# Two dense stages whose last round is handed over tile by tile, with other warming products on TensorE

## What is computed

```python
# block 1
x = x + g1 * (merged @ w_out[l])
h2 = rms_norm(x, norm2_gain[l]) * (1.0 + sc2) + sh2
x = x + g2 * moe_ffn(h2, w_router[l], ...)      # 32 experts, top 4 of 32, 1024 -> 2x1024 -> 1024
...
# block 2
x = x + merged @ w_out[l]
h2 = rms_norm_2(x, norm_ffn_g[l]).reshape(B * S, D)
y = hierarchical_moe(h2, ...)                   # 4 groups of 8 experts, top 1 group, top 2 inside, 1024 -> 256 -> 1024
x = x + y.reshape(B, S, D)
```

## Time and profile before

| what | value |
|---|---|
| median of three runs | 1577.53 us |
| lowest and highest of them | 1576.42 and 1578.69 us |
| span of the profiled execution | 1575.5 us |
| TensorE busy | 1455.8 us (92%) |
| VectorE, ScalarE busy | 602.0 us (38%), 339.3 us (22%) |
| mean granted TensorE clock | 0.985 |
| read from HBM | 592.66 MB, 377 GB/s over the span |

### The profile page before, as it was taken

One profiled execution on the slowest core, in us unless ns is written; L12 is line 12 of the kernel. 1 busy time (PEld: TensorE's weight loads), 2 busy tenths in 40 slices (PEclk: granted clock), 3 DMA queues, 4 the chain that ended last, 5 costly groups with the idle time before them and its releaser, 6 DMA issues.

```text
span 1575.5 us, 20915 instructions
## 1 busy us (share of the span) xinstructions
PE 1455.8 (92%) x8704; PEld 758.2 (48%) x8704; DVE 602.0 (38%) x911; ACT 339.3 (22%) x391; POOL 20.8 (1%) x33
## 2 busy tenths in 40 slices
PE   5999999999999999999999999999989999997677
PEld 2878985333333333333333333333348999753343
DVE  4686683232222231322313223223257587322111
ACT  4564432010101110101101001011033474221110
POOL 2100100000000000000000000000000000000000
PEclk9999999999999999999999999999999999998899
DMA  9976599999999999999999999999985437899997
GB/s 382 366 262 265 197 357 379 428 428 428 427 429 427 428 429 427 428 428 428 427 428 429 425 429 428 428 430 427 429 331 190 169 124 295 358 421 422 422 422 315
DMA packets 76733, 594.59 MB, mean 377 GB/s; under 512 B 5354, under 2 KB 6592, under 8 KB 37252
## 3 DMA queue, kind: packets, MB, share of 16 engines
q1 hardware_dynamic: 74416, 588.25, 90.4%
q0 software_dynamic: 1728, 4.86, 1.0%
q10 hardware_dynamic: 532, 0.64, 0.1%
HBM read 592.66 MB, written 1.06 MB: 377 GB/s over the span
## 4 chain that ended last, share of the span: by engine, by line
PE 50%; DMA 42%; DVE 6%; issue 1%; ACT 1%; SPq 0%; DVEq 0%; ACTq 0%
PE PS L539 45%; DMA ring<-in_w_up 32%; DMA ring<-in_w_gate_e 7%; PE PS L708 3%; DMA ring<-in_w_ada 1%; DMA arena<-in_w_in 1%; DVE ring_r L349 1%; PE PS L732 1%; PE PS L648 0%; DVE arena L807 0%; PE PS L1456 0%; ACT ring_r L344 0%; DVE arena_r L349 0%; PE PS L568 0%; DVE arena L2010 0%
## 5 line engine op out<-in xcount | busy, mean ns | idle before, releaser
L539 PE MATMUL PS<-ring,arena 128*64 128x512 f32 x3020 | 670.8, 596 | 46.2 <-DMA ring<-in_w_up 38.5
L539 PEld LDWEIGHTS PS<-ring,arena 128*64 128x64 f32 x3020 | 209.8, 137 | 469.5 <-issue 389.1
L539 PE MATMUL PS<-arena 128*128 128x128 f32 (+12 forms) x1240 | 227.6, 441 | 4.8 <-ACT arena L535 1.4
L795 DVE TENSOR_SCALAR arena<-PS 128x512 f32<-128x512 f32 x32 | 22.1, 692 | 487.6 <-PE PS L539 487.6
L539 PE MATMUL PS<-ring_r 128*128 128x256 f32 (+1 forms) x576 | 171.4, 305 | 0.4 <-DVE ring_r L1935 0.3
L518 ACT ACTIVATE arena<-arena 128x512 f32<-128x512 f32 x32 | 20.2, 630 | 703.3 <-DVE arena L795 703.3
L539 PEld LDWEIGHTS PS<-arena 64*128 64x128 f32 (+6 forms) x1240 | 108.4, 165 | 121.8 <-issue 114.4
L539 PE MATMUL PS<-hT_r,ring_r 128*128 128x256 f32 x800 | 151.4, 285 | 1.1 <-DVE ring_r L349 1.1
L349 DVE TENSOR_TENSOR ring_r<-ring,ring_r 128x2048 fp32r<-128x2048 f32 x51 | 116.4, 2291 | 39.3 <-ACT ring_r L344 38.2
L539 PEld LDWEIGHTS PS<-hT_r,ring_r 128*128 128x128 f32 x800 | 127.4, 193 | 3.2 <-issue 2.3
L344 ACT ACTIVATE ring_r<-ring 128x2048 fp32r<-128x2048 f32 x51 | 97.2, 1911 | 103.5 <-PE PS L539 98.5
(11 more groups left out here) (374 smaller groups left out, 974.8 us busy)
## 6 DMA issues: line engine op xcount, KB each, us to landing
ring<-in_w_up SPq DMA_DIRECT2D x128, 2048.0 KB, 23.2
ring<-in_w_down SPq DMA_DIRECT2D x59, 2048.0 KB, 21.6
ring<-in_w_in SPq DMA_DIRECT2D x17, 2048.0 KB, 11.2
ring<-in_w_gate_e SPq DMA_DIRECT2D x14, 2048.0 KB, 20.9
ring<-in_w_up_e SPq DMA_DIRECT2D x14, 2048.0 KB, 19.6
ring<-in_w_down_e SPq DMA_DIRECT2D x14, 2048.0 KB, 20.2
ring<-in_w_ada SPq DMA_DIRECT2D x12, 2048.0 KB, 15.9
ring<-in_w_out SPq DMA_DIRECT2D x4, 2048.0 KB, 7.7
```

Source lines behind the costliest of these rows:

```text
L539: return nc.tensor.matmul(o, w, m, start=first, stop=last)
L795: V.tensor_scalar(glu.rearrange("p (kk b q) -> p kk b q", kk=4, b=2), hu[:, :, :, :, 0], 7.0, None, ALU.min)\
```

## The change

It touches the end of both dense stages. The last round gives tile 0 to VectorE as soon as tile 0's products are done; the transposes of the first half move between the products of tile 0 and those of tile 1; the second half goes tile by tile through product, sum, gain, transposes, root and copies. Four warming products go in two places of the first tail, four in one place of the second, and there two wide and four short ones become seven short. The third group of position sums goes to bank 4 and gets a signal of its own.

```diff
@@ semaphores
+        OUT_ENDS = (R2 - 1, len(ROUNDS) - 1)
-            return S("half_done"), 1 + sum(1 for p in PIECES[:n] if not p[1])
+            return S("half_done"), 1 + sum(1 for p in PIECES[:n] if not p[1]) + (n >= M0)
+        def first_tile_done(r):
+            return S("half_done"), piece_used(pieces_of(r)[0])[1] + 1
@@ TensorE, split_tokens
+                        if r in OUT_ENDS and last and i == 0:
+                            ins.then_inc(S("half_done"), 1)
+                            after_first()
@@ TensorE, transposes in place of transpose_half
+        def transpose_first(pe, n):
+            pe.wait_ge(S("h"), H_SEEN[n] + 1)
+            src = h if n == "n2" else z4
+            for i in range(TT):
+                for k in range(4):
+                    last = nc.tensor.transpose(PS[:, i, k * P:(k + 1) * P], src[:, i, k * P:(k + 1) * P], ident)
+            last.then_inc(S("h_transposed"), 1)
+        def transpose_second(pe, i, n):
+            pe.wait_ge(S("h"), H_SEEN[n] + 2 + i)
+            src = h if n == "n2" else z4
+            for k in range(4):
+                last = nc.tensor.transpose(PS[:, 2 + i, k * P:(k + 1) * P], src[:, i, (4 + k) * P:(5 + k) * P], ident)
+            last.then_inc(S("h_transposed"), 1)
@@ TensorE, first tail
-            split_tokens(15, merged1_low)
+            split_tokens(15, merged1_low, None, lambda: transpose_first(pe, "n2"))
-            transpose_half(pe, 0)
             pe.wait_ge(S("shift_products"), 1)
             mm(PS[:, 6, 480:512], C("ones"), shift_sums, True, True).then_inc(S("logits"), 1)
-            keep_warm_short(4, 7)
+            transpose_second(pe, 0, "n2")
             pe.wait_ge(S("hT_A"), 2)
             for i in range(TT):
                 router_mm(w_r1, NE, i, range(4))
-            transpose_half(pe, 1)
-            keep_warm_short(4, 7)
+            transpose_second(pe, 1, "n2")
@@ TensorE, second tail
-            transpose_half(pe, 0, "n4")
-            keep_warm_short(4, 7)
+            transpose_second(pe, 0, "n4")
...
-            transpose_half(pe, 1, "n4")
+            transpose_second(pe, 1, "n4")
...
-            keep_warm(2, 7)
-            keep_warm_short(4, 7)
+            keep_warm_short(7, 7)
@@ TensorE, positions_mm
-            mm(PS[:, 5, 64:96], C("before"), M[:, 1, :], False, True)
-            mm(PS[:, 5, 128:160], C("ones"), M[:, 0, :], True, False)
-            mm(PS[:, 5, 128:160], C("ones"), M[:, 1, :], False, True).then_inc(S("positions"), 1)
+            mm(PS[:, 5, 64:96], C("before"), M[:, 1, :], False, True).then_inc(S("positions"), 1)
+            mm(PS[:, 4, 128:160], C("ones"), M[:, 0, :], True, False)
+            mm(PS[:, 4, 128:160], C("ones"), M[:, 1, :], False, True).then_inc(S("positions"), 1)
@@ ScalarE, rms_end in place of rms_sums
+            for tile in range(TT):
+                act.wait_ge(S("x_ready"), X_SEEN[n] + 2 + tile)
+                square(1, tile)
+                if tile == 0:
+                    root(0)
+                second_half(tile)
+            root(1)
@@ VectorE, first tail, second half of the columns
+            c = slice(512, 1024)
+            for i in range(TT):
+                xt_i = xt[:, 512 * i:512 * (i + 1)]
+                wait(v, first_tile_done(15) if i == 0 else (S("big_done"), 16))
+                last = TV(xt_i, PS[:, banks(15).start + i, :], G1[:, c], ALU.mult)
...
+                sig(TV(x[:, i, c], x[:, i, c], xt_i, ALU.add), "x_ready")
+                sig(TV(h[:, i, c], x[:, i, c], A2[:, c], ALU.mult), "h")
+                if i == 0:
+                    mean("n2", 0)
+            for i in range(TT):
+                if i:
+                    mean("n2", 1)
+                inverse_root("n2", i)
+                v.wait_ge(S("h_transposed"), T_SEEN["n2"] + 2 + i)
+                L(STT(out=h[:, i, :], in0=h[:, i, :], scalar=sm("rs")[:, i:i + 1], in1=SH2, op0=ALU.mult, op1=ALU.add))
```

More of the change, by code:

```diff
@@ L484, in gate_sig, with rms_end, square, root @@
                 .then_inc(S("big_free_A"), 1)
-        def rms_sums(act, n, squares, between=None):
-            k = int(n[1])
-            nc.scalar.sqrt(sm("nm")[:, 0:1], C("ones")[:, 0:1])
[L491 to L505, removed]
+        def rms_end(act, n, squares, first_half, second_half):
+            def square(i, tile):
+                a = 4 * i + 2 * tile
+                nc.scalar.activation(squares[:, a:a + 2, :] if squares is not None else
+                                     PS[:, (0 if i else 4) + tile, :].rearrange("p (k n) -> p k n", k=2),
+                                     x[:, tile, 512 * i:512 * (i + 1)].rearrange("p (k n) -> p k n", k=2),
+                                     ACT.Square, accum_out=sm("ss")[:, 2 * i + tile:2 * i + tile + 1])\
+                    .then_inc(S("squares"), 1)
+            def root(tile):
+                act.wait_ge(S("mean_square"), RMS_SEEN[n] + 1 + tile)
+                nc.scalar.sqrt(sm("rs")[:, tile:tile + 1], sm("ss")[:, tile:tile + 1]).then_inc(S("rms"), 1)
+            nc.scalar.sqrt(sm("nm")[:, 0:1], C("ones")[:, 0:1])
+            act.wait_ge(S("x_ready"), X_SEEN[n] + 1)
+            for tile in range(TT):
+                square(0, tile)
+            act.wait_ge(S("h_transposed"), T_SEEN[n] + 1)
+            first_half()
+            if squares is None:
+                act.wait_ge(S("hT_A"), 2)
+            for tile in range(TT):
+                act.wait_ge(S("x_ready"), X_SEEN[n] + 2 + tile)
[4 more added lines that the diff above has]
+            root(1)
@@ new lines, in mean, with inverse_root @@
+            def mean(name, tile):
+                ss = sm("ss")
+                v.wait_ge(S("squares"), (5 if name == "n2" else 11) + tile)
+                L(TV(ss[:, tile:tile + 1], ss[:, tile:tile + 1], ss[:, 2 + tile:3 + tile], ALU.add))
+                sig(TS(ss[:, tile:tile + 1], ss[:, tile:tile + 1], 1.0 / D, EPS, ALU.mult, ALU.add), "mean_square")
+            def inverse_root(name, tile):
+                v.wait_ge(S("rms"), RMS_SEEN[name] + 1 + tile)
+                L(V.reciprocal(sm("rs")[:, tile:tile + 1], sm("rs")[:, tile:tile + 1]))
@@ L2432, in _, with scaled @@
             split_lower(v, M0 + 27)
[L2433 to L2441 removed]
+            c = slice(0, 512)
+            gain4 = at(A2MAP, "gain")
+            o = begin(R2 + 14)
+            sig(TV(x[:, :, c], x[:, :, c], o, ALU.add), "big_free_V")
+            sig(V.memset(sm("ang"), 0.0), "x_ready")
+            v.wait_ge(S("ffn_gain"), 16)
+            sig(TV(z4[:, :, c], x[:, :, c], bc_mid(gain4[:, c], TT), ALU.mult), "h")
+            c = slice(512, 1024)
+            for i in range(TT):
+                wait(v, first_tile_done(R2 + 15) if i == 0 else (S("big_done"), len(ROUNDS)))
+                sig(TV(x[:, i, c], x[:, i, c], PS[:, banks(R2 + 15).start + i, :], ALU.add), "x_ready")
+                sig(TV(z4[:, i, c], x[:, i, c], gain4[:, c], ALU.mult), "h")
+                if i == 0:
+                    mean("n4", 0)
+            sig(V.memset(sm("ang"), 0.0), "big_free_V")
+            def scaled(i):
+                inverse_root("n4", i)
+                v.wait_ge(S("h_transposed"), T_SEEN["n4"] + 2 + i)
+                return TS(h[:, i, :].rearrange("p (k q) -> p q k", k=KD), z4[:, i, :].rearrange("p (q k) -> p q k", k=KD),
+                          sm("rs")[:, i:i + 1], None, ALU.mult)
+            L(scaled(0))
+            v.wait_ge(S("h_transposed"), T_SEEN["n4"] + 3)
             sig(CP(hT[:, 4:8, P:256], PS[:, 3, :].rearrange("p (k n) -> p k n", n=P)), "hT_V")
[L2443 to L2446 removed]
+            mean("n4", 1)
+            L(scaled(1))
             logits(3, "b_r2", 36)
```

89 lines of the change are left out of this document (35 added, 54 removed).

## The result

| | kernel before | changed kernel |
|---|---|---|
| median | 1577.3 us (20 runs) | 1581.79 us (20 runs) |
| lowest and highest | 1574.68 and 1579.13 | 1575.43 and 1583.73 |
| ratio of the times, 95% interval | | 1.0028 [1.002, 1.0036] |
| profiled execution: time, span | span 1575.5 us | 1582.97 us, span 1581.1 us |

The change makes the kernel slower by 0.28%. The forecast was no change, 1577.4 us; the measured time lies inside its range and beyond the bound of 0.2%, on which the lower end of the interval lies. The runs of the changed kernel fall into two heaps: three lie at 1575.43, 1576.16 and 1576.85, and the other seventeen between 1580.5 and 1583.73. The runs of the kernel before form one heap. The profiled execution, at 1582.97 us, belongs to the seventeen.

A forecast was written before the change was run, and what follows sets the result against it. The prediction took the weight loads to bound both expert stages. First tail -1.0 and second tail +0.85 gave -0.15 us on the span of 1575.5; with runs 2.0 us above it, the forecast was 1577.4 us, range 1575.4 to 1582.5.

The forecast's parts named there:

- What bounds the kernel: Both expert stages: each ends when its stream of weight loads ends; first-tail gains count up to 4.6 us.
- First tail at full clock: End of the first dense stage: logits 0.70 us earlier, tail 1.0 us shorter, bounds 0.5 and 1.3.
- The load that waits for the dense end: SyncE's load issued at 234.44 in the first tail: moves 1.05 us later, counted as nothing.
- the hole: Pause in the weight loads behind the first tail: 4.6 us before, forecast 3.6 us after the change.
- Second tail: End of the second dense stage: transposes delay the dense products and loads by 1.05 us; net cost 0.85 us.
- 0.2 us given back: Second tail: faster work behind the dense products regains only 0.2 us, the loss at the second stage's first slot.
- The clock: First tail: forecast held it at 1.00; rivals had it fall for some 7 us (0.27) or longer (0.13).
- the rival to which it gave 0.27 and 0.13: Clock falls in the first tail: 1580.1 us if for some 7 us (0.27), 1583.3 if longer (0.13).
- the short case: First tail: clock low for 6.8 us, back when the gather starts; price 2.7 us, 1580.1 us; chance 0.27.
- The long case: First tail: clock stays low through the gather's 32 instructions, 3.2 us more, 1583.3 us; chance 0.13.
- Tile 0 early: First tail: VectorE does tile 0 2.8 us ahead; rival without it 1579.5 us, 0.06 with other small losses.
- both tails counting: Rival: TensorE bounds the second expert stage, so both tails' gains count, -1.0 - 4.0, 1572.5 us; chance 0.04.

The follow-up runs named there:

- e2: Changed kernel with both groups of four warming products put back in the first tail; 1577.21 us, ratio 1.0004.
- e7: Changed kernel with four warming products added in the first tail, only behind the transposes of tile 1; 1577.95 us, ratio 1.0.
- e8: Changed kernel with eight identity transposes in each of two first-tail places, ahead of tile 0's second-half transposes and behind tile 1's; 1577.5 us, ratio 1.0002.
- e11: Changed kernel with twelve warming products instead of seven between router and position sums of the first tail; 1577.18 us, ratio 1.0003.
- e3: Kernel before without its two groups of four warming products in the first tail, order by halves kept; 1582.02 us, ratio 1.0029.
- e10: Changed kernel with the second tail's first-half transposes moved behind the last dense product, no warming group back; 1582.07 us, ratio 1.0032.
- e1: Changed kernel with four warming products put back in the first tail, ahead of tile 0's second-half transposes; 1578.03 us, ratio 1.0009.

## Why the prediction was wrong

**What bounds the kernel: right.** Both expert stages end with their streams of loads. The whole loss of the first tail passes through to the end: +4.25 at the first slot's load, +5.6 at the end of the span with the second tail's share.

**First tail at full clock: right.** Forecast were 0.70 us at the logits and 1.0 us in all. Without a fall the tail measures 17.89 to 18.09 us, with 1.05 added 18.94 to 19.14, against 19.94 before: 0.8 to 1.0 us shorter. These are kernels with warming products added (e2, e7, e8, e11); the changed kernel itself wasn't profiled without a fall. The load that waits for the dense end was costed at nothing, with the hole as its cover, and the cover held, since this sum is counted at the end of the hole. Something was lost ahead of it: 344 GB/s in the window 236 to 240 us of the changed kernel and 381 in e11, against 430 before. In e11 the hole itself, reckoned as in the prediction, was (276 + 10 + 6) x 4 / 428 = 2.7 us, and 0.4 us more were lost in that window; forecast were 3.6.

**Second tail: right.** Forecast was +1.05 for the dense end, measured +0.95; forecast were 0.2 us given back, and the rest of the stage showed none (+0.16), which is within what executions differ. TensorE's first expert products came 2.7 us sooner after the loads (17.0 against 19.7), where 3 to 4 had been named.

**The clock: wrong, and with it the result.** The forecast's sum put the removed warming products of the first tail at nothing, "as long as the clock stays up", and gave that case its chance of 0.50 on the sentence "TensorE is never idle for long in this stretch". That is the step that failed. Taking the eight products out of the kernel before, and nothing else, costs 4.5 us of the median (e3); putting them back into the changed kernel brings it to 1577.21 (e2); in the profile of the changed kernel the lower clock costs 6.3 us. The sign that the prediction had named for its being wrong, a clock under 1.00 between 238 and 250 us, is what the profile shows, and the rival to which it gave 0.27 and 0.13 fits the seventeen slower runs of twenty, of which one was profiled.

The sentence on the idle time fails on two counts. The prediction's own numbers held a gap: the router done near 240.7 plus 1.8 us of warming products ends at 242.5, with the position sums at 243.15. The real gap was 1.46 us in place of these 0.65, mostly since TensorE finished the router 0.7 us sooner than worked out. And the second tail before, which was set against this stretch as one with long idle time, had none as long. The longest gap that its timeline shows ahead of the fall was

```profile
1352.42 2.80 PE L539 MATMUL PS<-small,hT 128*128 128x36 f32 x16 [0.69 <-ACT hT L1350]
```

Nor had the first tail "two more such groups" than the second: it had two groups of four, the second tail one.

**Its price: the short case was too low, the long one near by offsetting errors.** The short case took its 6.8 us at the lower level from the second tail. Behind the first tail's fall the clock stayed low for 13.7 us, through the gather, the bias and part of the first expert's first products. The growths are 6.93 - 3.98 = 2.95, 5.75 - 3.65 = 2.1 (3.65 in e11 and before), 1.20 - 0.71 = 0.5 and 1.63 - 0.92 = 0.7 us: 6.25 of the 6.3 us. The long case, 1583.3 us, was near: the seventeen runs lie at 1580.5 to 1583.7. Its 2.7 + 3.2 = 5.9 us come close to 6.3 in part by luck: it had left out the bias and the first expert's products (2.6 us), counted 1.1 us for the seven warming products, which were done before the clock fell, and 1.6 for the position sums and the three warming products, where 0.8 were lost.

How long a fall lasts isn't explained by the wide warming products of the second tail before. The changed kernel and e7 have the same order there, with seven short products and no wide one. In the changed kernel's profile the clock was low there for 10.2 us (0.50, 0.50 and 0.72 in the windows from 1356 to 1368), in that of e7 for (0.20 + 0.22) x 4 / 0.5 = 3.4 us:

```profile
1348.00:1352.00 4.00, 3.38 (x24) 3.27 (x24) 3.49 (x8) 1.49 (x2) 0.00 (x0) 0.80 1.00 422
1352.00:1356.00 4.00, 3.43 (x23) 3.14 (x23) 3.07 (x21) 0.26 (x1) 0.00 (x0) 0.78 1.01 426
```

What a microsecond at the lower level costs can be read from the first tails: 6.3 us for 13.7 and 22.62 - 17.89 = 4.7 for 10.2 (e10), but only 18.55 - 17.89 = 0.7 for 3.4 in e1, where the warming products that grew stood for the most part in TensorE's waiting time.

**Tile 0 early, and both tails counting: right to be small.** VectorE takes tile 0 at 230.84, 3.7 us ahead of tile 1. The expert stage behind the second tail took no notice of starting 2.7 or 4.8 us sooner.

What remains open: how much of the fall is due to idle time and how much to narrow products, and what sets when it begins and how long it lasts. e1 fell without idle time and e11 held with the narrow stretch, each in its profiled execution. The split of the position sums was not tried alone; in the traces the selection follows the sums' start after 0.97 us instead of 1.41.

## What to carry to other kernels

A warming product in a place where the engine isn't late can cost next to nothing (here the first tail is 18.09 us with both groups and 17.89 with one), and its removal must be costed like that of any other instruction: ask what TensorE does in the microseconds around it, and what the work behind it would take at the lower clock. Work taken off TensorE leaves idle time where the chain on the other engines doesn't get shorter by as much (1.46 us in the changed kernel, next to none with both groups back), so each removal has to be checked for the gap that it leaves. And when a transfer or a stage's end waits for the last product of a round, nothing should be put ahead of that product unless the transfer has a cover.

## What was not expected of the hardware

In the changed kernel's profile TensorE did 4.9 us of products of 32 columns and transposes and 1.8 us of warming products, was idle for 1.46 us, and the granted clock fell 1.1 us into the position sums. It stayed down for 13.7 us although TensorE was busy in all of them, through the gather's 32 instructions of 64 columns, and rose again near 257 us, among the first expert's 16 instructions of 512 columns (window 256 to 260 us: 0.88). With the same first tail it fell 2.6 us after the idle time in e10 and stayed down for 10.2 us. In e1 it fell with no idle time at all and came back after 3.4 us, within products of 128 and 32 columns; in e3 it stayed down for 20.5 us.

The times of one kernel can so spread into two heaps, as they do here. Time alone doesn't tell in which executions the clock fell: the profiled execution of e1 had a fall and took 1578.98 us, and the kernel before has runs as long.

Eight transposes in the place of four warming products held the clock in both kernels (1576.89 and 1577.5 us, no window under 1.00 in the first tail of either profiled execution). The Trainium skill (TensorE: Matmul & The Clock Gate, Part 4: PE-mode transpose) says that a transpose doesn't count for the clock as a product does; in these float32 runs, with products on either side of the transposes, the measurement says otherwise.
